# State updates of a gated linear recurrence: one 128-row matmul over block-masked values, or four matmuls on 32-row bands

## What is computed

```python
N = S // C                      # S = 256 tokens, C = 32: 8 chunks, H = 8 heads, D = 128
k_end = kh * jnp.exp(b_last[:, :, :, None, :] - bcum)
U = jnp.einsum('bhnsd,bhnsv->bhndv', k_end, ih)
decay = jnp.exp(b_last)
def step(state, xs):
    d, u = xs
    return d[..., None] * state + u, state
```

## Time and profile before

| what | value |
|---|---|
| median of 3 runs | 1722.16 us (1721.86 to 1722.63) |
| profiled execution: span from first to last instruction | 1714.9 us |
| profiled execution: its own time | not recorded apart; its span is 7.3 us below the median of the runs |
| TensorE busy | 1690.7 us, 99% of the span |
| VectorE, ScalarE, GpSimd busy | 1111.8 us, 778.0 us, 265.3 us |
| mean granted TensorE clock | 0.998 of full speed |
| recurrence | about 305 to 523 us of the span |

### The profile page before, as it was taken

How to read it: one execution, slowest core, us unless ns; L and a number is a source line. 1 busy time by engine, 2 the same in 40 slices (tenths; PEclk the granted TensorE clock), 3 DMA queues, 4 the chain that set the end, 5 groups by cost and what they waited for, 6 DMA issues and landing times.

```text
span 1714.9 us, 26652 instructions
## 1 busy us (share of the span) xinstructions
PE 1690.7 (99%) x9668; PEld 1470.7 (86%) x9668; DVE 1111.8 (65%) x1141; ACT 778.0 (45%) x891; POOL 265.3 (15%) x169
## 2 busy tenths in 40 slices
PE   7999999999999999999999999999999999999998
PEld 6888888888888888888888888888888888888887
DVE  5766697777785665556765666666666666665554
ACT  6633434455454344344533345544554544444332
POOL 0000050110114520045100000000000005600164
PEclk9999999999999999999999999999999999999999
DMA  8566755554554554447566565555555555554353
GB/s 286 184 187 188 229 180 171 164 160 146 158 161 148 188 180 130 152 135 244 161 189 190 185 195 168 155 176 175 171 171 169 169 164 176 181 167 151 119 189 110
DMA packets 291924, 296.65 MB, mean 173 GB/s; under 512 B 8992, under 2 KB 288800, under 8 KB 291616
## 3 DMA queue, kind: packets, MB, share of 16 engines
q1 hardware_dynamic: 291872, 295.94, 55.1%
HBM read 293.81 MB, written 2.10 MB: 173 GB/s over the span
## 4 chain that ended last, share of the span: by engine, by line
PE 97%; DVE 1%; DMA 1%; ACT 0%; SPq 0%; issue 0%; DVEq 0%; ACTq 0%
PE ps L258 59%; PE ps L260 30%; PE ps L350 2%; PE ps L333 2%; PE ps L412 1%; PE ps L440 1%; DMA xv<-mem 1%; DVE wpair L780 0%; PE ps L481 0%; PE ps L472 0%; PE ps L491 0%; PE ps L391 0%; PE ps L280 0%; PE ps L342 0%; PE ps L437 0%; DVE tmp L799 0%
## 5 line engine op out<-in xcount | busy, mean ns | idle before, releaser
L780 DVE TENSOR_TENSOR wpair<-raw,wpair 128x1024 fp32r<-128x1024 f32 x544 | 711.0, 1320 | 380.6 <-ACT wpair L541 372.9
L541 ACT ACTIVATE wpair<-raw 128x1024 fp32r<-128x1024 f32 x544 | 571.6, 1058 | 727.0 <-PE ps L260 718.1
L258 PE MATMUL ps<-xpair,wpair 128*128 128x512 f32 x1920 | 684.7, 400 | 0.0
L258 PE MATMUL ps<-ypair,wpair 128*128 128x512 f32 x1536 | 539.6, 396 | 4.8 <-DVE ypair L867 3.0
L260 PE MATMUL ps<-xpair,wpair 128*128 128x256 f32 x1920 | 536.9, 280 | 0.0
L258 PEld LDWEIGHTS ps<-xpair,wpair 128*128 128x128 f32 x1920 | 360.5, 188 | 85.8 <-issue 1.7
L260 PE MATMUL ps<-ypair,wpair 128*128 128x256 f32 x1536 | 428.6, 279 | 0.0
L260 PEld LDWEIGHTS ps<-xpair,wpair 128*128 128x128 f32 x1920 | 362.2, 189 | 2.1 <-issue 1.7
L258 PEld LDWEIGHTS ps<-ypair,wpair 128*128 128x128 f32 x1536 | 288.4, 188 | 73.8 <-issue 6.0
L260 PEld LDWEIGHTS ps<-ypair,wpair 128*128 128x128 f32 x1536 | 289.7, 189 | 0.3 <-issue 0.2
L799 DVE TENSOR_REDUCE tmp<-ps 128x512 f32<-128x1024 f32 x136 | 166.2, 1222 | 65.9 <-PE ps L260 65.5
(11 more groups left out here) (179 smaller groups left out, 986.8 us busy)
## 6 DMA issues: line engine op xcount, KB each, us to landing
raw<-xa_wkv SPq DMA_DIRECT2D x128, 512.0 KB, 4.2
raw<-w_in_odd SPq DMA_DIRECT2D x128, 512.0 KB, 3.9
raw<-w_in_even SPq DMA_DIRECT2D x96, 512.0 KB, 3.6
raw<-xa_wq SPq DMA_DIRECT2D x64, 512.0 KB, 3.6
raw<-xa_wo SPq DMA_DIRECT2D x64, 512.0 KB, 3.6
raw<-w_out_even SPq DMA_DIRECT2D x32, 512.0 KB, 4.0
raw<-w_out_odd SPq DMA_DIRECT2D x32, 512.0 KB, 4.5
xv<-mem SPq DMA_DIRECT2D x8, 512.0 KB, 8.1
```

The source lines that it names most:

```text
L258: mm(bank, still[:, k, 0, tile], move[:, k].rearrange("p h n -> p (h n)"), start=(k == 0), stop=False)
L541: fn(wpair[:, KP * p:KP * (p + 1), 0, :], raw[:, p], ACT.Copy).then_inc(hi_ready, 1)
L780: v.tensor_tensor(wpair[:, kp, 1, :], raw[:, p], wpair[:, kp, 0, :].bitcast(F32), ALU.subtract).then_inc(lo_ready, 1)
```

## The change

- `hg_bd`, its mask `chunk_mask` (4 columns of the constants) and GpSimd's two multiplications are gone, with the semaphore `hg_bd_ready`.
- TensorE waits for `hg_values` in its place, besides the key copy.
- Each matmul over 128 rows becomes four over 32 rows. Band n takes rows 32n to 32n + 31 of the keys and of the unmasked values, 128 moving columns, at the array's row position 32n, and writes bank 4 + n. With four values of a that is 16 matmuls in place of 4.
- The banks change their meaning (bank = chunk within the tile, column = a), and VectorE's reads follow.

```diff
-                  ("hg_mask", P), ("reset", S), ("chunk_mask", P // HC)):
+                  ("hg_mask", P), ("reset", S)):
...
-        hg_bd = view(0, 2, 4, CH)
...
                 def chunk_updates():
                     pe.wait_ge(s["hg_kcopy"], it + 1)
-                    pe.wait_ge(s["hg_bd_ready"], it + 1)
+                    pe.wait_ge(s["hg_values"], it + 1)
                     for a in range(4):
                         h, t = a // 2, a % 2
-                        last = mm(ps[:, 4 + a, :], hg_ken[:, a, :], hg_bd[:, t, :, h * P:(h + 1) * P],
-                                  start=True, stop=True)
+                        for n in range(P // HC):
+                            rows = slice(n * HC, (n + 1) * HC)
+                            last = mm(ps[:, 4 + n, a * P:(a + 1) * P], hg_ken[rows, a, :],
+                                      hg_i[rows, t, h * P:(h + 1) * P], start=True, stop=True,
+                                      skip_group_check=True, tile_position=(n * HC, 0))
                     last.then_inc(s["hg_u"], 1)
...
-                            u = ps[:, 4 + 2 * h + n // 4, (n % 4) * P:(n % 4 + 1) * P]
+                            a = 2 * h + n // 4
+                            u = ps[:, 4 + n % 4, a * P:(a + 1) * P]
...
             with pool.Fori(0, 4, 1) as it:
-                pool.wait_ge(s["hg_values"], it + 1)
-                pool.wait_ge(s["hg_keys"], it + 1)
-                for t in range(2):
-                    last = g.tensor_tensor(hg_bd[:, t], hg_i[:, t, :].unsqueeze(1).to_broadcast([P, 4, CH]),
-                                           const("chunk_mask").unsqueeze(2).to_broadcast([P, 4, CH]), ALU.mult)
-                last.then_inc(s["hg_bd_ready"], 1)
                 pool.wait_ge(s["hg_gsig"], it + 1)
...
-        "chunk_mask": p // HC == np.arange(P // HC)[None, :],
```

More of the change, by code:

```diff
@@ L161, in build @@
             lb_a lb_b lb_c lb_d lb_ready prod_ready cs_ready diff_ready diff_scaled mixed_ready pool_g pool_sig_ready pool_gs pool_mm pool_y
-            y_hi hg_logit hg_sig hg_f0 hg_f1 hg_logf hg_bcum hg_exps hg_d hg_kexp hg_keys hg_ktr hg_kcopy hg_values hg_bd_ready
+            y_hi hg_logit hg_sig hg_f0 hg_f1 hg_logf hg_bcum hg_exps hg_d hg_kexp hg_keys hg_ktr hg_kcopy hg_values
             hg_u hg_state hg_query hg_scores hg_scores_m hg_omm hg_osq hg_norm hg_r0 hg_r1 hg_gate hg_gsig hg_gg0 hg_gg1 hg_y0 hg_y1
```

## The result

The changed kernel took 1711.01 us (median), against 1722.16 before: a ratio of 0.9926 with a 95% interval of 0.9902 to 0.995. Four of its five executions lie between 1703.78 and 1711.45 us; the fifth took 2390.8 us at a mean granted clock of 0.654 and is left out of the ratio. Measured again later beside the kernel before it was 1705.79 against 1718.11, ratio 0.9932 (0.9915 to 0.995). The ratios are those on record with their intervals; they are not the quotients of the medians, which are 0.9935 and 0.9928 here and differ by up to 0.0014 in the experiments. So the kernel is faster by 0.7%, some 12 us, and outside the forecast's range on the low side. The forecast of no change was wrong, and rival A, the only faster one, had the right sign but was too small as well.

What follows compares the result with a forecast made beforehand. TensorE's stream, busy 99% of the span, was taken as the bound. Per iteration 3.55 + 0.17 - 3.43 = +0.29 us, +1.2 us in four, added to the 1722.16 us median: 1723.3 us, range 1716.0 to 1728.0.

Steps and rivals of the forecast that it cites:

- rival A: L412 group: bands run beside each other, paced by 16 records, saving 5.9 us in all, 1716.3 us; chance 0.38.
- What bounds the kernel: Whole kernel: TensorE's stream, busy 99% of the span; L412 costs 3.43 us per iteration, 13.7 us in all.
- The masking: GpSimd's two multiplications, 5.58 us per iteration: removal costed at almost nothing, because L412 hardly waits for them.
- VectorE's time: L780 conversions beside the masking: 2.3 us per iteration come back, some 9 us in all, costed at nothing.
- the moved wait: L412's wait goes to hg_values, whose L1020 ends 8.6 us before L412: costs nothing.
- the states: VectorE's PSUM reads after the group: first starts 5.1 us after L412's last matmul, still about 5 us behind afterwards.
- The wait showing through: L412 start in iteration 1: 0.08 us may be waiting for masking; 0.3 us at most in four, left out.
- The price of a narrow record: L412 group: 0.111 us per record of 128 columns with its own weight load, so 32 cost 3.55 us.
- The switch: Either side of the L412 group: going from whole array to bands and back, 0.17 us taken, between 0 and 0.7.
- B: L412 group: bands in single file, as forecast, 1723.3 us, own range 1722.0 to 1725.5; chance 0.40.
- Rival C: L412 group: a band's second weight load isn't hidden, 8.0 us slower in all, 1730.2 us; chance 0.22.
- The constants' load: Early in the kernel: 4 columns shorter out of more than 1000, costed at nothing.

Runs made afterwards that it cites:

- band after band: Changed kernel with the loops swapped, so four matmuls run on one band, then four on the next: 1715.67 us, ratio 0.9967 against the kernel before.

## Why the prediction was wrong

**What bounds the kernel: right.** TensorE's stream was and is the bound, 3.43 us per iteration of L412 was the right stake (3.43 in iteration 0; 3.52 in the mean with the little wait), and only what came off it counted.

**The masking, VectorE's time, the moved wait, the states: right.** The run without masking gave 0.9995 (0.9983 to 1.0007). VectorE got 12.3 us back and not 9, and none of it counted. The wait showing through was worth 0.4 us, where I had allowed 0.3 and left it out.

**The price of a narrow record: right as a price, wrong for bands.** 128-row matmuls of 128 columns cost 0.111 us each, as read from L421. The step that failed is "with bands one after the other the group is 32 x 0.111 = 3.55 us". Measured, the group costs 1.65 - 0.35 = 1.30 us: 8 steps of 0.111 and 0.41 for switching. That is 2.2 us less than before per iteration, where the sum had 0.29 us more. L440 was the misleading row: it showed that loads don't overlap with one another, but all of its loads were for the whole array. For loads on disjoint rows it proved nothing, and I let it weigh against A.

**Rival A: the right mechanism, too small.** Its step "The group is then paced by 16 rather than 32 records" assumed that the next band starts only when the band before it has issued its second record, in program order. The changed kernel starts four at a time: each band is a line of its own with 8 records, so 8 x 0.111 = 0.89 us and not 1.78. The second page that I cited, "TensorE: Matmul & The Clock Gate" of the Trainium skill (Part 3), was on the right side: it has about 4 ns from one start to the next, and the trace shows some 7 ns. No row of before could show this, since none of its matmuls leaves rows free.

**The switch: mis-sized.** I took 0.17 us per visit between 0 and 0.7; it measured 0.36 to 0.41. The forecast's own range for B is also uneven: its +0.5 us would give 1722.7, and 1722.0 needs records of 0.107 us.

**Rival C: didn't occur.** With 0.111 us from one record of a band to the next, its second load is hidden like any other, but for the first step of a visit (0.21 us).

**The constants' load: wrong at "nothing".** I costed the 4 columns as a transfer and didn't think of what their removal moves. It was worth 0.26% (0.0016 to 0.0035), about a third of the gain, and why stays open. It isn't what broke the range: the group alone gives 1722.2 - 8.9 = 1713.3 us, already below 1716.0.

## What to carry to other kernels

fp32 matmuls that contract over 32 rows and move 128 columns cost a quarter (0.89 us against 3.57 for 32 records) when four neighbours in the program use four different bands and PSUM banks; with the same band four times in a row, most of that is lost. Band and bank changed together in all these runs, so bands that share a bank are not tested. A visit to bands costs TensorE about 0.4 us, so group them. And when a kernel is compared at the level of a quarter of a percent, check whether the edit moved tensors or changed their size: rerun the old kernel with only that.

## What the hardware showed that was not expected

- Bands overlap with their weight loads too: 32 loads and 32 matmuls in 1.17 us, where the same number over 128 rows takes 3.73.
- Work on another band is started ahead of waiting work, but only a few records ahead: band after band, about three of a band's eight steps were covered.
- A steady stream of the same pairs has two paces, 0.347 and 0.353 us in the mean, at the same full granted clock. It keeps one of them for long stretches. In one stretch of 350 us the pace went with the four columns of the constants in all twelve profiles. In other stretches it differs between executions of the same kernel too (the changed kernel's two profiles got 397 and 405 pairs through between 860 and 1000 us), a likely part of the spread of single executions (before: 1714.9 to 1726.5 us over all runs).
- The changed kernel's profiled execution has stretches at half the granted clock in the middle of busy work, which that of before lacks until its end. The windows view shows two of them as means of 0.83 and 0.79:

```profile
458.00:468.00 10.00, 10.00 (x54) 8.52 (x54) 2.80 (x4) 3.97 (x6) 0.00 (x0) 0.83 0.32 101
509.00:517.00 8.00, 8.00 (x44) 6.88 (x44) 1.22 (x1) 2.71 (x5) 0.60 (x2) 0.79 0.29 89
```

  TensorE was busy throughout both. Whether bands favour them is open: before the one at the very end, the seven profiles of kernels with bands have one to three such stretches, and the five without have one or none.
